# Sixteen pairs of seven block products per layer in place of thirteen, with a third buffer set, in a two-layer decoder trunk

## Chip, cores, metric

The kernel runs on one core of a Trainium2 chip. The metric is the device time of one execution in microseconds. The three timed executions of the kernel before gave 2402.96, 2403.00 and 2404.28 us (median 2403.0).

## What is computed

Two layers over 256 tokens of width 1024. Each layer has a mixer (an input projection, sparse attention with a compressed branch, a gated linear recurrence, a state-space mixer, merge gates, an output projection), and then a retrieval over 128 x 128 single-neuron experts. Cut to what the change touches:

```
x = x + hybrid_mixer(rms_norm(x), ...)
x = x + peer_ffn(rms_norm(x), w_q, sub_keys, u, v)

# inside the mixer, compressed branch:
#   hidden = gelu(blocks @ w1)        (15 blocks a group, 256 hidden columns)
#   k_cmp, v_cmp = hidden @ w2

# peer_ffn: top 16 of 128 x 128 keys for each of 8 heads, gates g
act = gelu(u[eidx] . h)
out = sum over chosen experts of (g * act) * v[eidx]
```

The kernel computes the experts densely. For every token it spreads the gates over all 128 x 128 experts, so that the last product is acts (256 tokens x 16384 experts, mostly zero) times v (16384 x 1024).

## The kernel before

**Products in three passes.** All large products are float32 split in a high and a low part; a product is three matmuls (high by high, high by low, low by high). ScalarE (ACT) makes the high part by a copy with rounding, VectorE (DVE) or GpSimd (POOL) the low part by a subtraction. TensorE (PE) waits for the low part.

**The value stage** is the last stage of a layer. acts times v is cut in 128 units of 128 experts. A plain unit (`value`) is 12 matmuls of 128x512: two token tiles, two column halves, three passes. Its v block comes over `x_load` on the SP queue (512 KB; five slots in turn, so that the load of unit i+4 of the plain units waits until i units are multiplied), then `x_hi` on ACT, then `x_lo` on DVE. The activations of two units are split by `p_hi_pair` and `p_lo_pair`. ACT and DVE each run a loop over i in which they prepare unit i+3; in the loops, every second i begins with a pair split, which on ACT waits until i units are multiplied.

**Seven block products.** A pair of units is a 2 x 2 block matrix product (2 token tiles x 2 units) by (2 units x 2 column halves). For the pairs named in `SEVEN` it is made with seven block products in place of eight: `seven(j)` is 21 matmuls of 128x512 in place of 24. For it four v quarters are loaded (`b_load`, 256 KB each), ACT makes `b_high` and `sums_high`, `a_high`, `a_sums_high`; DVE makes `first_sums`, `last_sums`, `b_low`, `a_sums`, `sums_low`, `a_low`. Tuples such as `FIRST_SUMS` say at which i of the loops each is done, and `SEVEN_AT` before which plain unit PE does the pair. The buffers lie over activations that are used up. Pairs 0 to 2 use set 0 alone (they follow each other at 14 plain units), the others alternate between sets 1 and 0, four plain units apart. `seven_sums`, six steps of DVE at the six plain units after the last pair, add the PSUM banks of the block products to `x`.

There are 13 such pairs a layer and 102 plain units; the last pair comes before plain unit 82.

**The end of layer 0.** SP also issues the first weights of layer 1: `load_first(1)`, the gains, `load_first(0)` and `load_first_rest` (512 KB, the second half of the first weight unit). ACT splits the first unit at the plain unit of number 120 (`one_by_one(120)`, i = 94 of 102), ahead of that i's `x_hi`, and waits there for both halves; DVE makes its low part at i = 96, ahead of that i's `x_lo`. The second unit follows at i = 98 (ACT) and i = 100 (DVE). PE does the last three plain units for token tile 0 first, then `add_sums(0)` on DVE opens the next layer.

**The compressed branch in the mixer.** PE turns the hidden layer (four transposes), does half a unit of projection and eight transposes of q, and then waits for `chT` and `chV`, the turned hidden layer, copied out by ACT. ACT does before that copy: the high part of unit XBC+2, the high part of XBC+3, the copy out of unit XBC+1, and the high part of XBC+4, for which it waits for a load.

Of the kernel before, what the change touches and what calls it, by code (L numbers as in the profile page):

```python
# [24 lines left out]
F32 = mybir.dt.float32  # L25
I32 = mybir.dt.int32
U32 = mybir.dt.uint32
F32R = mybir.dt.float32r
# [82 lines left out]

SEVEN = (7, 15, 23, 26, 29, 32, 35, 38, 41, 44, 47, 50, 53)
SEVEN_SET = (0, 0, 0, 1, 0, 1, 0, 1, 0, 1, 0, 1, 0)
PLAIN = tuple(i for i in range(NKEY) if i // 2 not in SEVEN)
ONE_BY_ONE = len(PLAIN)
SEVEN_AT = tuple(2 * r - 2 * j for j, r in enumerate(SEVEN))
# [13 lines left out]
def slot_free(m):  # L132
# [17 lines left out]
    "seven_loaded_0": 64 * SEVEN_SET.count(0), "seven_loaded_1": 64 * SEVEN_SET.count(1), "seven_hi": 4 * len(SEVEN),  # L150
# [69 lines left out]
def trunk(nc, x_in, pos_tok, pos_row, const, wstream, small, rows, mix_row, ffn_row, subkeys, xstream, out):  # L220
    V, A, PE, PO = nc.vector, nc.scalar, nc.tensor, nc.gpsimd
    with ExitStack() as ctx:
# [3 lines left out]
        def sem(name):  # L226
            return ctx.enter_context(nc.semaphore(name))
# [85 lines left out]
        s_bl = [sem(f"seven_loaded_{i}") for i in range(2)]  # L313
# [7 lines left out]
        def layer_programs(layer):  # L321
# [6 lines left out]
            def past(s):  # L328

                return layer * PER_LAYER[s.name]  # L330
# [133 lines left out]
            with mix:  # L464
# [55 lines left out]
                with mid:  # L520
# [520 lines left out]
                    def mixer_scalar(act):  # L1041
# [106 lines left out]
                        for j in range(2):  # L1148
                            ge = A.activation(chid[j], bank[7][CHAT[j], 0:S], ACT.Gelu_apprx_tanh)
                        ge.then_inc(s_chg, 1)  # L1150
                        for n in range(2, 4):
                            split_hi(act, XBC + n)
                        filler(XBC + 1)
                        act.wait_ge(s_cht, past(s_cht) + 1)
                        A.activation(chT[:], bank[7][:, 0:2 * CROWS].rearrange("p (k c) -> p k c", k=2), ACT.Copy)
                        for k in range(2):
                            for g in range(G):
                                at = k * CROWS + 16 * g
                                rep = A.activation(chV[:, k, g], times(bank[6][:, at:at + NCMP], 8), ACT.Copy)
                        rep.then_inc(s_chtev, 1)  # L1160
                        act.wait_ge(s_cksq, past(s_cksq) + 1)
                        A.activation(kst[:, 0:2], kst[:, 0:2], ACT.Sqrt, scale=1 / DH).then_inc(s_ckrt, 1)
                        filler(XBC + 2)
# [212 lines left out]
                    def mixer_vector(dve):  # L1376
# [165 lines left out]
                        for k in range(CONV):  # L1542
                            lru_conv(k, 0)
                            if k == 0:
                                half_lo(dve, XBC + 1)
                            elif k == 2:
                                split_lo(dve, XBC + 2)
                                q_taken(0)
                                q_taken(1)
                        lru_conv(0, 1)  # L1550
                        split_lo(dve, XBC + 3)

                        dve.wait_ge(s_co, past(s_co) + 1)
                        own = cst[0:8 * NCMP, C_HEAD:C_HEAD + 8].rearrange("p (a g) -> p a g", g=G)
# [537 lines left out]
            with ExitStack() as tmp:  # L2092
# [13 lines left out]
                           for q in range(4)]  # L2106

                unit_at = [acts_at + 4 * i * S for i in range(NKEY)]
                raw_at, sums_at = (feat_at, unit_at[6]), (feat_at + 4 * KT * S, unit_at[14])
                high_at, part_at = (hot_at + 4 * 4 * S, unit_at[22]), (unit_at[0], unit_at[36])  # L2110
                assert high_at[0] + 4 * 7 * 512 <= acts_at
                b_raw = [alias(f"b_raw_{i}", [P, 4, 512], F32, offset=raw_at[i]) for i in range(2)]
                b_lo = [alias(f"b_lo_{i}", [P, 4, 512], F32R, offset=raw_at[i]) for i in range(2)]
                b_sum = [alias(f"b_sum_{i}", [P, 4, 512], F32, offset=sums_at[i]) for i in range(2)]
                b_sum_lo = [alias(f"b_sum_lo_{i}", [P, 4, 512], F32R, offset=sums_at[i]) for i in range(2)]
                b_hi = [alias(f"b_hi_{i}", [P, 7, 512], F32R, offset=high_at[i]) for i in range(2)]
                a_hi = [alias(f"a_hi_{i}", [P, 4, P], F32R, offset=part_at[i]) for i in range(2)]
                a_sum_hi = [alias(f"a_sum_hi_{i}", [P, 4, P], F32R, offset=part_at[i] + 16 * P) for i in range(2)]
                a_sum = [alias(f"a_sum_{i}", [P, 4, P], F32, offset=part_at[i] + 32 * P) for i in range(2)]
                a_sum_lo = [alias(f"a_sum_lo_{i}", [P, 4, P], F32R, offset=part_at[i] + 32 * P) for i in range(2)]  # L2120

                NS = len(SEVEN)
                SHARED = tuple(j == 0 or SEVEN_SET[j] == SEVEN_SET[j - 1] for j in range(NS))
                OTHER_FREE = sum(i < 42 for i in PLAIN)
                OTHER_AFTER = sum(2 * r < 42 for r in SEVEN)
# [12 lines left out]

                def one_by_one(unit):

# [71 lines left out]
                def expert_sync(sp):  # L2212
# [7 lines left out]
                    for m in range(XR, VU + ONE_BY_ONE):  # L2220
                        x_load(sp, m)
                        done = m - XV + 1 - VU
                        if done in (1, 2):
                            sp.wait_ge(s_xu, past(s_xu) + VU + done)
                            for piece in range(2 * done - 2, 2 * done):
                                b_load(0, piece)
                        if done in (OTHER_FREE, OTHER_FREE + 1):
                            sp.wait_ge(s_xu, past(s_xu) + VU + OTHER_FREE)
                            sp.wait_ge(s_bmul, past(s_bmul) + OTHER_AFTER)
                            for piece in range(2 * (done - OTHER_FREE), 2 * (done - OTHER_FREE) + 2):  # L2230
                                b_load(SEVEN_SET.index(1), piece)
# [108 lines left out]
                def expert_scalar(act):  # L2340
# [64 lines left out]
                    def b_high(j):  # L2405

                        b = SEVEN_SET[j]
                        act.wait_ge(s_bl[b], past(s_bl[b]) + 64 * (SEVEN_SET[:j].count(b) + 1))
                        A.activation(b_hi[b][:, 0, :], b_raw[b][:, 0, :], ACT.Copy)
                        A.activation(b_hi[b][:, 1:3, :], b_raw[b][:, 2:4, :], ACT.Copy).then_inc(s_bhi, 1)  # L2410
# [59 lines left out]
                def expert_vector(dve):  # L2470
# [129 lines left out]
                    def first_sums(j):  # L2600

                        b = SEVEN_SET[j]
                        w = b_raw[b]
                        dve.wait_ge(s_bl[b], past(s_bl[b]) + 64 * (SEVEN_SET[:j].count(b) + 1))
                        dch.link(V.tensor_tensor(b_sum[b][:, 0:2, :], w[:, 1:4:2, :], w[:, 0:2, :], ALU.subtract))

# [15 lines left out]
                    def a_sums(j):  # L2622

                        b, unit = SEVEN_SET[j], 2 * SEVEN[j]
                        if j == 0:
                            dve.wait_ge(s_xu, past(s_xu) + VU + 6)
                        a11, a21, a12, a22 = [acts[:, unit + n, t * P:(t + 1) * P] for n in range(2) for t in range(2)]
                        s1, s2, s3, s4 = [a_sum[b][:, n, :] for n in range(4)]
                        dch.add(V.tensor_tensor(s1, a21, a22, ALU.add))
# [234 lines left out]
```

## Time and profile before

| | |
|---|---|
| median of three executions | 2403.0 us |
| profiled execution, its own time | 2402.95 us |
| its span in the trace | 2401.1 us |
| granted TensorE clock, mean | 0.999 of full |
| PE busy | 2379.0 us (99%) |
| DVE busy | 1911.3 us (80%) |
| ACT busy | 1444.8 us (60%) |
| POOL busy | 791.3 us (33%) |
| DMA queue q1 | 416.47 MB, 51.2% of 16 engines |

The difference between the execution's own time and its span (1.85 us) lies around the program. PE busy is no measure of speed, since matmuls overlap and their ends are modelled; the distance from one matmul's start to the next is what counts. The tables below are rows of the page, of the chain of work that ended last, of the timelines of single engines and of the DMA issues. In a timeline a line has its start, its duration, the engine, the line of the kernel, the operation with output and inputs, and in brackets how long the engine was idle before it and who released it.

### The profile page before, as it was taken

The numbers are of one execution on the slowest core, as the hardware profiler recorded it, in microseconds if no ns is written. First come the engines' busy times: TensorE is split into PE (matmuls) and PEld (weight loads), VectorE is DVE, ScalarE is ACT, GpSimd is POOL, SyncE is SP. The second block draws the span as 40 slices with busy tenths as digits, with TensorE's granted clock in tenths as the row PEclk, the third lists the DMA queues.
The fourth block names the chain that finished last, engine by engine and source line by source line (L and its number), as shares of the span: only waits on it lengthen the run. The fifth ranks groups of instructions, "written<-read, shape, count | busy, mean of one in ns | idle before, by whom it ended". The sixth has DMA issues, their size and how long they took to land.

```text
span 2401.1 us, 43695 instructions
## 1 busy us (share of the span) xinstructions
PE 2379.0 (99%) x17453; PEld 2215.8 (92%) x17453; DVE 1911.3 (80%) x3222; ACT 1444.8 (60%) x2123; POOL 791.3 (33%) x452
## 2 busy tenths in 40 slices
PE   9999999999999999999999999999999999999999
PEld 8999999999999988888899999999999999888887
DVE  7988787499389985899779886865984899868995
ACT  6587664444577764665555966644446777656663
POOL 0011310288888820000000113003888989100000
PEclk9999999999999999999999999999999999999999
DMA  7633335355544466666555333453555444566664
GB/s 258 221 124 124 112 140 197 132 185 185 178 159 161 162 204 198 214 201 224 183 193 211 124 124 117 150 184 139 184 180 175 159 161 160 204 203 211 200 192 150
DMA packets 104169, 419.26 MB, mean 175 GB/s; under 512 B 11680, under 2 KB 12192, under 8 KB 87072
## 3 DMA queue, kind: packets, MB, share of 16 engines
q1 hardware_dynamic: 103968, 416.47, 51.2%
q8 instruction: 140, 2.29, 0.4%
q14 instruction: 61, 0.50, 0.1%
HBM read 415.38 MB, written 1.05 MB: 173 GB/s over the span
## 4 chain that ended last, share of the span: by engine, by line
PE 90%; DVE 4%; ACT 3%; DMA 2%; issue 1%; POOL 1%; SPq 0%; DVEq 0%; ACTq 0%
PE banks L2306 23%; PE banks L421 18%; PE banks L422 18%; PE banks L423 18%; PE banks L2287 3%; PE banks L2322 2%; PE banks L2323 2%; PE banks L2321 2%; DVE ring_lo L396 1%; PE banks L881 1%; DMA ring<-in_wstream 1%; POOL xr_lo L1902 1%; DMA xr<-in_xstream 1%; PE banks L768 1%; PE banks L839 1%
## 5 line engine op out<-in xcount | busy, mean ns | idle before, releaser
L1902 POOL TENSOR_TENSOR xr_lo<-xr,xr_hi 128x1024 fp32r<-128x1024 f32 x256 | 621.0, 2429 | 388.0 <-ACT xr_hi L1896 386.7
L1896 ACT ACTIVATE xr_hi<-xr 128x1024 fp32r<-128x1024 f32 x420 | 442.7, 1055 | 282.9 <-DMA xr<-in_xstream 282.2
L421 PE MATMUL banks<-featH,xr_hi 128*128 128x256 f32 x2048 | 576.3, 281 | 1.8 <-POOL xr_lo L1902 1.8
L422 PE MATMUL banks<-featL,xr_hi 128*128 128x256 f32 x2048 | 575.3, 281 | 0.0
L423 PE MATMUL banks<-featH,xr_lo 128*128 128x256 f32 x2048 | 575.2, 281 | 0.0
L421 PEld LDWEIGHTS banks<-featH,xr_hi 128*128 128x128 f32 x2048 | 385.7, 188 | 2.6 <-POOL xr_lo L1902 1.7
L423 PEld LDWEIGHTS banks<-featH,xr_lo 128*128 128x128 f32 x2048 | 386.1, 189 | 0.0
L422 PEld LDWEIGHTS banks<-featL,xr_hi 128*128 128x128 f32 x2048 | 386.1, 189 | 0.0
L421 PE MATMUL banks<-featH,ring_hi 128*128 128x256 f32 x1232 | 351.0, 285 | 2.2 <-DVE ring_lo L396 2.1
L422 PE MATMUL banks<-featL,ring_hi 128*128 128x256 f32 x1232 | 346.2, 281 | 0.0
L423 PE MATMUL banks<-featH,ring_lo 128*128 128x256 f32 x1232 | 345.9, 281 | 0.0
L1317 POOL TENSOR_TENSOR tok_z<-tok_z,rst 128x512 f32<-128x512 f32 (+1 forms) x32 | 51.0, 1593 | 822.1 <-DVE rst L1620 822.1
L396 DVE TENSOR_TENSOR ring_lo<-ring,ring_hi 128x2048 fp32r<-128x2048 f32 x118 | 270.8, 2298 | 58.5 <-ACT ring_hi L388 57.2
L388 ACT ACTIVATE ring_hi<-ring 128x2048 fp32r<-128x2048 f32 x118 | 225.2, 1911 | 90.9 <-PE banks L423 73.2
L1902 DVE TENSOR_TENSOR xr_lo<-xr,xr_hi 128x1024 fp32r<-128x1024 f32 x164 | 200.5, 1222 | 58.2 <-ACT xr_hi L1896 57.4
L421 PEld LDWEIGHTS banks<-featH,ring_hi 128*128 128x128 f32 x1232 | 232.3, 189 | 5.4 <-issue 4.2
L422 PEld LDWEIGHTS banks<-featL,ring_hi 128*128 128x128 f32 x1232 | 232.2, 188 | 0.1
L423 PEld LDWEIGHTS banks<-featH,ring_lo 128*128 128x128 f32 x1232 | 232.2, 188 | 0.0
L2306 PE MATMUL banks<-xr_lo,p_hi 128*128 128x512 f32 x656 | 202.8, 389 | 0.0
L2306 PE MATMUL banks<-xr_hi,p_hi 128*128 128x512 f32 x656 | 202.7, 389 | 0.0
L2306 PE MATMUL banks<-xr_hi,acts_lo 128*128 128x512 f32 x656 | 202.7, 389 | 0.0
L2566 DVE TENSOR_TENSOR hot<-banks,choice 128x1024 fp32r<-128x1024 f32 x128 | 156.6, 1224 | 53.5 <-PE banks L2287 51.6
(424 smaller groups left out, 4962.3 us busy)
## 6 DMA issues: line engine op xcount, KB each, us to landing
xr<-in_xstream SPq DMA_DIRECT2D x420, 512.0 KB, 3.3
ring<-in_wstream SPq DMA_DIRECT2D x128, 1024.0 KB, 4.8
b_raw<-in_xstream SPq DMA_DIRECT2D x104, 256.0 KB, 3.4
xv<-in_xstream SPq DMA_DIRECT2D x40, 512.0 KB, 4.3
smw<-in_small SPq DMA_DIRECT2D x4, 617.0 KB, 9.3
first<-in_wstream SPq DMA_DIRECT2D x4, 512.0 KB, 5.9
first<-in_wstream SPq DMA_DIRECT2D x2, 1024.0 KB, 7.7
subk<-in_subkeys SPq DMA_DIRECT2D x2, 1024.0 KB, 7.0
```

The source lines that it names most:

```text
L388: A.activation(hi, w, ACT.Copy).then_inc(s_hi, 1)
L396: V.tensor_tensor(lo, w, hi.bitcast(F32), ALU.subtract).then_inc(s_lo, 1)
L421: PE.matmul(o, s_hi_lo[0], m_hi_lo[0], start=first, stop=False)
L422: PE.matmul(o, s_hi_lo[0], m_hi_lo[1], start=False, stop=False)
L423: return PE.matmul(o, s_hi_lo[1], m_hi_lo[0], start=False, stop=last)
L1317: PO.tensor_tensor(sc[:, n % 2, :, 0:nk], sc[:, n % 2, :, 0:nk], over(rst[:, n % 2, 2, :], nk), ALU.mult).then_inc(s_scaled, 1)
L1896: A.activation(hi, w, ACT.Copy).then_inc(s_xhi, 1)
L1902: (PO if m < NKEY else V).tensor_tensor(lo, w, hi.bitcast(F32), ALU.subtract).then_inc(s_xlo_pool if m < NKEY else s_xlo_dve, 1)
L2287: mm = PE.matmul(gate_bank(g)[:, 2 * j * P:2 * (j + 1) * P], hots(g)[:, j, 0, :], hots(g)[:, j, 1:3, :], start=True, stop=True)
L2306: mm = PE.matmul(bank[2 * t + h][:], p, w[:, h * 512:(h + 1) * 512], start=first_one and i == 0, stop=last and i == ONE_BY_ONE - 1)
L2321: PE.matmul(bank[o][:], p[0], w[0], start=o >= 4 and j == 0, stop=False)
L2566: V.tensor_tensor(hots(g)[:, :, 0:3:2, :], iota.unsqueeze(1).unsqueeze(1).to_broadcast([P, GB, 2, NKEY]), choice[:, 0:2, GB * g:GB * (g + ...
```

## The change

Sixteen pairs in place of thirteen: pairs follow each other at ten plain units while set 0 is alone (7, 13, 19), then at four (from pair 22). There are 96 plain units, and the last pair comes before plain unit 86. The last pair has a buffer set of its own (set 2). The steps of preparation get places counted from the pair before (`step(alone, start, in_turn)`) in place of `lead`; waits (`used_up`) guard the buffers that now lie over other activations. The loads of the first weights of layer 1 are tied to other pairs. In the compressed branch, ACT copies the turned hidden layer before it splits XBC+3 and XBC+4, and DVE makes the low part of XBC+3 before a step of the recurrence's convolution.

```diff
-SEVEN = (7, 15, 23, 26, 29, 32, 35, 38, 41, 44, 47, 50, 53)
-SEVEN_SET = (0, 0, 0, 1, 0, 1, 0, 1, 0, 1, 0, 1, 0)
+SEVEN = (7, 13, 19, 22, 25, 28, 31, 34, 37, 40, 43, 46, 49, 52, 55, 58)
+SEVEN_SET = (0, 0, 0, 1, 0, 1, 0, 1, 0, 1, 0, 1, 0, 1, 0, 2)
...
                         ge.then_inc(s_chg, 1)
-                        for n in range(2, 4):
-                            split_hi(act, XBC + n)
-                        filler(XBC + 1)
+                        split_hi(act, XBC + 2)
+                        take(XBC + 1, xbcT[:, 2:4, PAD:])
                         act.wait_ge(s_cht, past(s_cht) + 1)
...
                         rep.then_inc(s_chtev, 1)
+                        split_hi(act, XBC + 3)
+                        next_hi(XBC + 1)
                         act.wait_ge(s_cksq, past(s_cksq) + 1)
...
+                        split_lo(dve, XBC + 3)
                         lru_conv(0, 1)
-                        split_lo(dve, XBC + 3)
...
-                raw_at, sums_at = (feat_at, unit_at[6]), (feat_at + 4 * KT * S, unit_at[14])
-                high_at, part_at = (hot_at + 4 * 4 * S, unit_at[22]), (unit_at[0], unit_at[36])
+                raw_at, sums_at = (feat_at, unit_at[6], unit_at[22]), (feat_at + 4 * KT * S, unit_at[14], unit_at[81])
+                high_at = (hot_at + 4 * 4 * S, unit_at[22], unit_at[89])
+                part_at = (unit_at[0], extra_at + 10 * D, unit_at[66])
...
-                def lead(j, units, later):
-
-                    return SEVEN_AT[j] - units if SHARED[j] else SEVEN_AT[j - 1] + later
-
-                B_HIGH = FIRST_SUMS = tuple(lead(j, 11, -2) for j in range(NS))
-                LAST_SUMS = tuple(lead(j, 10, -1) for j in range(NS))
-                SUMS_HIGH = tuple(lead(j, 9, -1) for j in range(NS))
-                B_LOW = tuple(lead(j, 8, -1) for j in range(NS))
-                A_HIGH = A_SUMS = tuple(lead(j, 7, 0) for j in range(NS))
-                A_SUMS_HIGH = SUMS_LOW = tuple(lead(j, 6, 0) for j in range(NS))
-                A_LOW = tuple(lead(j, 4, 0) for j in range(NS))
+                OTHER = SEVEN_SET.index(1)
+
+                def step(alone, start, in_turn):
+
+                    return tuple(SEVEN_AT[0] - 11 + alone if j == 0 else SEVEN_AT[j - 1] + alone if j < OTHER else
+                                 SEVEN_AT[j - 1] + (start if j == OTHER else in_turn) for j in range(NS))
+
+                FIRST_SUMS, B_HIGH = step(1, -2, -2), step(1, -1, -2)
+                LAST_SUMS, SUMS_HIGH = step(2, -1, -1), step(2, 0, -1)
+                B_LOW, A_HIGH, A_SUMS = step(3, 0, -1), step(4, 0, 0), step(4, 0, 0)
+                A_SUMS_HIGH, SUMS_LOW, A_LOW = step(5, 1, 0), step(5, 1, 0), step(6, 1, 0)
+
+                def used_up(eng, unit):
+
+                    eng.wait_ge(s_xu, past(s_xu) + VU + sum(i < unit for i in PLAIN))
+                    eng.wait_ge(s_bmul, past(s_bmul) + sum(2 * r < unit for r in SEVEN))
...
-                            if SEVEN_SET[j] in SEVEN_SET[j + 1:]:
+                            if j + 2 < NS and j + 1 >= OTHER or j + 1 < OTHER:
                                 sp.wait_ge(s_bmul, past(s_bmul) + j + 1)
                                 for piece in range(4):
-                                    b_load(SEVEN_SET.index(SEVEN_SET[j], j + 1), piece)
+                                    b_load(j + 2 if j + 1 >= OTHER else j + 1, piece)
                         if layer + 1 < L:
-                            if done == SEVEN_AT[NS - 1] + 2:
+                            if done == SEVEN_AT[NS - 2] + 2:
                                 programs[layer + 1]["load_first"](sp, 0)
-                            elif done == SEVEN_AT[NS - 1] + 4:
+                            elif done == SEVEN_AT[NS - 1] + 2:
                                 programs[layer + 1]["load_first_rest"](sp)
```

`done` is the number of plain units multiplied. `load_first_rest` is issued at done = 86 of 102 before and at done = 88 of 96 after; ACT splits the first unit at i = 94 of 102 before and at i = 88 of 96 after, DVE at i = 96 and i = 90. The six steps of `seven_sums` lie at i = 83 to 88 before and at i = 87 to 92 after.

## Rows read from the trace of the kernel before

**Rows 1.** Page, part 4: the chain that ended last, by engine.

```profile
PE 90%; DVE 4%; ACT 3%; DMA 2%; issue 1%; POOL 1%; SPq 0%; DVEq 0%; ACTq 0%
```

**Rows 2.** The chain in order of time, value stage of layer 0 (start, us, what).

```profile
863.60 38.09 PE banks L2306 x168
...
992.49 10.91 PE banks L2306 x48
...
1149.52 50.37 PE banks L2306 x222
```

**Rows 3.** Timeline of PE, compressed branch, layer 0 and then layer 1.

```profile
94.05 1.09 PE L744 MATMUL banks<-cst,tok_q 128*128 128x128 f32 x8
94.90 0.36 PE L421 MATMUL banks<-featH,ring_hi 128*128 128x256 f32 x1
...
104.35 1.04 PE L744 MATMUL banks<-cst,tok_q 128*128 128x128 f32 x8
105.45 0.62 PE L792 MATMUL banks<-smw,xbcC 128*15 128x64 f32 x8
...
1297.01 1.04 PE L744 MATMUL banks<-cst,tok_q 128*128 128x128 f32 x8
1298.25 0.62 PE L792 MATMUL banks<-smw,xbcC 128*15 128x64 f32 x8 [0.20 <-ACT xbcC L1159]
```

**Rows 4.** Timeline of ACT, compressed branch, layer 0.

```profile
100.89 0.60 ACT L1075 ACTIVATE xbcT<-banks 128x512 f32<-128x512 f32 x1
102.73 1.92 ACT L388 ACTIVATE ring_hi<-ring 128x2048 fp32r<-128x2048 f32 x1 [1.24 <-DMA ring<-in_wstream]
...
104.65 0.75 ACT L1159 ACTIVATE xbcC<-banks 128x120 f32<-128x120 f32 x4
```

**Rows 5.** Timeline of the SP queue, end of layer 0.

```profile
1118.14 1.75 SPq L2216 DMA_DIRECT2D b_raw<-in_xstream  x4
...
1160.46 0.33 SPq L1886 DMA_DIRECT2D xr<-in_xstream  x1
1160.83 1.20 SPq L364 DMA_DIRECT2D first<-in_wstream  x1
```

**Rows 6.** DMA issues of short windows: KB each, us from issue to landing.

```profile
first<-in_wstream SPq DMA_DIRECT2D x1, 512.0 KB, 5.7
...
first<-in_wstream SPq DMA_DIRECT2D x1, 512.0 KB, 4.4
...
b_raw<-in_xstream SPq DMA_DIRECT2D x2, 256.0 KB, 3.8
```

**Rows 7.** Timeline of ACT, value stage of layer 0.

```profile
1133.55 1.92 ACT L2416 ACTIVATE b_hi<-b_sum 128x2048 fp32r<-128x2048 f32 x1 [4.46 <-DVE b_sum L2612]
...
1182.77 1.90 ACT L388 ACTIVATE first_hi<-first 128x2048 fp32r<-128x2048 f32 x1
1184.57 1.04 ACT L1896 ACTIVATE xr_hi<-xr 128x1024 fp32r<-128x1024 f32 x1
```

**Rows 8.** Timeline of DVE, value stage of layer 0.

```profile
1122.37 0.28 DVE L2629 TENSOR_TENSOR a_sum<-acts 128x128 f32<-128x128 f32 x1
...
1123.43 2.29 DVE L2638 TENSOR_TENSOR b_sum_lo<-b_sum,b_hi 128x2048 fp32r<-128x2048 f32 x1
...
1160.63 0.68 DVE L2665 TENSOR_TENSOR x<-x,banks 128x512 f32<-128x512 f32 x1
...
1161.94 0.69 DVE L2597 TENSOR_TENSOR acts_lo<-acts,p_hi 128x512 fp32r<-128x512 f32 x1
1162.55 1.22 DVE L1902 TENSOR_TENSOR xv_lo<-xv,xv_hi 128x1024 fp32r<-128x1024 f32 x1
1163.68 0.68 DVE L2668 TENSOR_TENSOR x<-x,banks 128x512 f32<-128x512 f32 x1
...
1189.35 2.28 DVE L396 TENSOR_TENSOR first_lo<-first,first_hi 128x2048 fp32r<-128x2048 f32 x1
...
1199.91 1.29 DVE L2714 TENSOR_TENSOR x<-x,banks 128x512 f32<-128x512 f32 x2 [0.59 <-PE banks L2306]
```

More of the change, by code:

```diff
@@ L149 @@
     "expert_weights_loaded_4": 16 * slot_loads(4),
-    "seven_loaded_0": 64 * SEVEN_SET.count(0), "seven_loaded_1": 64 * SEVEN_SET.count(1), "seven_hi": 4 * len(SEVEN),
+    "seven_loaded_0": 64 * SEVEN_SET.count(0), "seven_loaded_1": 64 * SEVEN_SET.count(1), "seven_loaded_2": 64 * SEVEN_SET.count(2),
+    "seven_hi": 4 * len(SEVEN),
     "seven_made": 3 * len(SEVEN), "seven_multiplied": len(SEVEN),
@@ L312, in trunk @@
         s_phi, s_plo, s_xffn = sem("probs_hi"), sem("probs_lo"), sem("x_ffn")
-        s_bl = [sem(f"seven_loaded_{i}") for i in range(2)]
+        s_bl = [sem(f"seven_loaded_{i}") for i in range(3)]
         s_bhi, s_bmade, s_bmul = sem("seven_hi"), sem("seven_made"), sem("seven_multiplied")
@@ L2108, in layer_programs @@
                 unit_at = [acts_at + 4 * i * S for i in range(NKEY)]
-                raw_at, sums_at = (feat_at, unit_at[6]), (feat_at + 4 * KT * S, unit_at[14])
-                high_at, part_at = (hot_at + 4 * 4 * S, unit_at[22]), (unit_at[0], unit_at[36])
-                assert high_at[0] + 4 * 7 * 512 <= acts_at
-                b_raw = [alias(f"b_raw_{i}", [P, 4, 512], F32, offset=raw_at[i]) for i in range(2)]
-                b_lo = [alias(f"b_lo_{i}", [P, 4, 512], F32R, offset=raw_at[i]) for i in range(2)]
@@ L2114, in layer_programs @@
[L2114 to L2118, printed above, removed]
@@ L2119, in layer_programs @@
-                a_sum = [alias(f"a_sum_{i}", [P, 4, P], F32, offset=part_at[i] + 32 * P) for i in range(2)]
-                a_sum_lo = [alias(f"a_sum_lo_{i}", [P, 4, P], F32R, offset=part_at[i] + 32 * P) for i in range(2)]
-                NS = len(SEVEN)
-                SHARED = tuple(j == 0 or SEVEN_SET[j] == SEVEN_SET[j - 1] for j in range(NS))
-                OTHER_FREE = sum(i < 42 for i in PLAIN)
-                OTHER_AFTER = sum(2 * r < 42 for r in SEVEN)
-                def lead(j, units, later):
-                    return SEVEN_AT[j] - units if SHARED[j] else SEVEN_AT[j - 1] + later
@@ new lines, in layer_programs @@
+                high_at = (hot_at + 4 * 4 * S, unit_at[22], unit_at[89])
+                part_at = (unit_at[0], extra_at + 10 * D, unit_at[66])
+                a_sum_at = (unit_at[0] + 32 * P, unit_at[36], unit_at[66] + 32 * P)
+                assert high_at[0] + 4 * 7 * 512 <= acts_at and part_at[1] + 32 * P <= extra_at + 15520
+                b_raw = [alias(f"b_raw_{i}", [P, 4, 512], F32, offset=raw_at[i]) for i in range(3)]
+                b_lo = [alias(f"b_lo_{i}", [P, 4, 512], F32R, offset=raw_at[i]) for i in range(3)]
@@ new lines, in layer_programs @@
+                b_sum = [alias(f"b_sum_{i}", [P, 4, 512], F32, offset=sums_at[i]) for i in range(3)]
+                b_sum_lo = [alias(f"b_sum_lo_{i}", [P, 4, 512], F32R, offset=sums_at[i]) for i in range(3)]
+                b_hi = [alias(f"b_hi_{i}", [P, 7, 512], F32R, offset=high_at[i]) for i in range(3)]
+                a_hi = [alias(f"a_hi_{i}", [P, 4, P], F32R, offset=part_at[i]) for i in range(3)]
+                a_sum_hi = [alias(f"a_sum_hi_{i}", [P, 4, P], F32R, offset=part_at[i] + 16 * P) for i in range(3)]
@@ new lines, in layer_programs @@
+                a_sum = [alias(f"a_sum_{i}", [P, 4, P], F32, offset=a_sum_at[i]) for i in range(3)]
+                a_sum_lo = [alias(f"a_sum_lo_{i}", [P, 4, P], F32R, offset=a_sum_at[i]) for i in range(3)]
+                NS = len(SEVEN)
+                OTHER = SEVEN_SET.index(1)
+                def step(alone, start, in_turn):
+                    return tuple(SEVEN_AT[0] - 11 + alone if j == 0 else SEVEN_AT[j - 1] + alone if j < OTHER else
+                                 SEVEN_AT[j - 1] + (start if j == OTHER else in_turn) for j in range(NS))
@@ L2226, in expert_sync @@
                                 b_load(0, piece)
[L2227 to L2231, printed above, removed]
+                        other = done - SEVEN_AT[OTHER - 1] + 6
+                        if other in (0, 1):
+                            used_up(sp, 14)
+                            for piece in range(2 * other, 2 * other + 2):
+                                b_load(OTHER, piece)
                         if done in SEVEN_AT:
@@ L2407, in b_high @@
                         b = SEVEN_SET[j]
+                        if j == OTHER:
+                            used_up(act, 36)
+                        elif b == 2:
+                            used_up(act, 103)
                         act.wait_ge(s_bl[b], past(s_bl[b]) + 64 * (SEVEN_SET[:j].count(b) + 1))
@@ L2603, in first_sums @@
                         w = b_raw[b]
+                        if j == OTHER:
+                            used_up(dve, 22)
+                        elif b == 2:
+                            used_up(dve, 89)
                         dve.wait_ge(s_bl[b], past(s_bl[b]) + 64 * (SEVEN_SET[:j].count(b) + 1))
@@ L2626, in a_sums @@
                             dve.wait_ge(s_xu, past(s_xu) + VU + 6)
+                        elif j == OTHER:
+                            used_up(dve, 38)
                         a11, a21, a12, a22 = [acts[:, unit + n, t * P:(t + 1) * P] for n in range(2) for t in range(2)]
```

## The prediction, on record before the result

> **What bounds the kernel now.** I read the page's chain first: nine tenths of it are PE [rows 1], so a saving is real only if it shortens PE's own work, and a delay elsewhere counts only where it makes PE wait. Then I followed the chain through the value stage of layer 0. The reader is to see there that nothing but matmuls stands between its start and its end, and that the starts are regular: from 863.60 to 992.49 there are three rounds of 14 plain units and one pair, 42.96 us each; from 992.49 to 1149.52 ten rounds of 4 units and one pair, 15.70 us each [rows 2]. The difference of 27.26 us is ten units, so a unit takes 2.726 us (the last run of 222 matmuls gives 50.37 / 222 x 12 = 2.72) and a pair of seven products 15.70 - 10.90 = 4.80 us. PE is the bound, and ACT, DVE and SP run ahead of it. The third reading is how far ahead, in the timelines of these engines.
>
> **More pairs.** Each new pair takes away two plain units (5.45 us) and adds 4.80 us: 0.65 us less. Three pairs in each of two layers: 6 x 0.65 = 3.9 us gained. The rows are regular over 13 rounds, so I give this term no range, on condition that PE never waits.
>
> **The turned hidden layer.** In layer 0 PE starts eight transposes at 104.35; the same eight took 0.85 us from start to the next work at 94.05. It could go on at 105.20 and does at 105.45; in layer 1 at 1297.86 and does at 1298.25, with ACT's copy named as releaser [rows 3]. ACT's copies end at 105.40 because they stand behind a high part that waited 1.24 us for its load and ran from 102.73 [rows 4]. In the new order they follow the copy out that starts at 100.89, and end near 102.5, well ahead. Gain 0.25 + 0.39 = 0.6 us, from both ends 0 (if the next wait takes it) to 0.6. I take 0.6, since the chain after it is PE's own. The high part of XBC+3 moves to about 102.5 to 104.4, its low part (2.29 us, as the same shape in [rows 8]) ends before 107, and PE, which goes on at 105.2, has 16 small matmuls and half a unit to do before it needs it. DVE only changes the order of two pieces of work. I cost these moves at nothing; without that cover each would cost at most the 1.9 us of the high part.
>
> **The end of layer 0.** This is where I expect the time to go. Count from the moment at which 88 plain units are multiplied. SP then issues a unit's load and, 0.37 us later, `load_first_rest`, as it did at 1160.46 and 1160.83 [rows 5]. That transfer took 5.7 us to land [rows 6], so it lands at 6.1. Before, ACT asked for it eight units after its issue; now ACT asks at i = 88, which it enters at the same moment as SP (its pair split waits for 88 units). So ACT stands from 0.6 to 6.1. Behind that wait are the high part of the first unit (1.80 us to the next instruction) and then `x_hi` of unit 91 (1.04 us) [rows 7]: ready at 8.95. DVE's low part takes 1.22 us [rows 8]: 10.2. PE wants unit 91 after three units, at 8.2. **Stall one: 2.0 us.**
>
> DVE is then late as well. From 1161.94, 1162.55 and 1163.68 a pair split takes 0.61 us and an `x_lo` 1.13 us before the next can start, and a step of `seven_sums` 1.31 us (1160.63 to 1161.94); the low part of the first unit takes 2.28 us [rows 8]. The six steps of `seven_sums` now fall on i = 87 to 92, together with that low part at i = 90. After `x_lo` of unit 91 starts at 9.0, unit 92 is ready at 9.0 + 1.13 + 1.31 + 1.22 = 12.7, in time for PE at 12.9. Unit 93 must wait for a step, a pair split and the low part: its `x_lo` starts at 11.4 + 1.13 + 1.31 + 0.61 + 2.28 = 16.8 and ends at 18.0, and PE wants it at 10.2 + 5.45 = 15.65. **Stall two: 2.3 us.** The last three units are done for tile 0 first, half a unit (1.36 us) each, while DVE needs 1.13 + 1.31 = 2.44 us for each: **stalls three and four, 1.1 us each.** Then a last step of sums and the low part of the second unit (another 2.28 us) stand before `add_sums(0)`: DVE is free at about 25.6 and PE's sums of tile 0 are there at 24.2. Before, `add_sums` started at 1199.91, where the last run of matmuls ends in the chain [rows 2, 8]. **A delay of 1.4 us** on the chain into layer 1. Together 2.0 + 2.3 + 1.1 + 1.1 + 1.4 = 7.9 us, in layer 0 only. The other landing of such a transfer was 4.4 us [rows 6], which takes 1.3 us off the first term: 6.6 us. Layer 1 has neither the load nor the splits, and I cost its end at nothing: without the wait DVE's work on i = 87 to 92 fits in the two units by which it is ahead.
>
> The Trainium skill (DMA: Bandwidth & Descriptors, section on the anatomy of one DMA) puts a transfer at about 2.0 us plus its bytes over 436 GB/s, 3.2 us for 512 KB. The two landings here, 5.7 and 4.4 us, are longer. By the page's figure ACT would be through at 6.5, unit 91 in time, and the end of the layer would cost about 5.5 us in place of 7.9, the whole sum 2.4 us less.
>
> **While set 0 is alone.** For pairs 1 and 2 the quarters can be loaded only when the pair before is multiplied, and the preparation now starts one unit after it and not three. Count from the end of that pair. Four issues take 1.75 us [rows 5], the last starts at 1.3 plus 0.2 for the semaphore, and lands 3.8 us later [rows 6]: 5.3. ACT's `b_high` (a p and an x shape, 1.5), pair split (0.5) and `x_hi` (1.04): 8.4. DVE's `x_lo` 1.22 and last sums 1.3: 11.0. ACT's `sums_high` 1.92 and next `x_hi` 1.04 [rows 7]: 13.95. From there DVE has no wait but much work: `x_lo` three times before the last (3.39), `b_low` 1.74, two pair splits 1.22, `a_sums` 1.06 (1122.37 to 1123.43), `sums_low` 2.2, and the `x_lo` of the ninth unit on 1.22 [rows 8]: 24.8. PE wants that unit after nine units, 24.5. That is 0.3, and with the semaphore steps I left out 0.4. Two such places in each layer: 1.6 us. From both ends: 0 if DVE is half a microsecond quicker, 0.9 us each (3.6) if the quarters land later. Pair 0 is prepared up to a unit earlier than it was but with the same work; layer 0's slower loads may add 0.3. In the stretch where sets alternate, the places of the work are those of before, and the rounds of 15.70 held; the third set only gives the last pair its own buffers, and its waits are for units used up long before. No cost.
>
> **Sum.** -3.9 - 0.6 + 7.9 + 1.6 + 0.3 = +5.3 us. The profiled execution took 2402.95 us, the median is 2403.0, so the sum is made against the same figure: 2408.3 us, 0.22% more. A change of 0.2% (4.8 us) is about what a measurement of this kernel tells from none.
>
> **Rivals.** *The end is cheap.* If the rest of the first weights lands before ACT needs it, or DVE makes its steps faster, only stalls two to four are left, or part of them: 4.5 + 1.6 + 0.3 + 0 to 2 - 4.5, between 2404 and 2406.5. For it speaks the 4.4 us landing, against it that DVE's part follows from its own rows. *No stall at the end and none between pairs* (the other side): PE then keeps its regular starts and the whole gain stays, 2403.0 - 4.5 = 2398.5, or 2400 with the 1.6. It decides from the point at which unit 91 is ready at 8.2, so the load must land by 4.1, and DVE must also be done with unit 93 by 13.6. Against it stands every row used above. *DVE and ACT become the bound.* A round of four units and one pair costs DVE nearly PE's 15.70 us; if the preparation of pairs 1 and 2 is later than I think, its delay is kept through all later rounds, each pair waits, and the upper ends hold (3.6 and more): 2410.5 to 2415. For it speaks that ACT and DVE wait for each other inside a round (4.46 us idle in [rows 7]), against it that in the 13 rounds of [rows 2] no pair waited.
>
> **Chances.** Forecast, 2406.5 to 2410.5: 0.57. Cheap end: 0.16. No stall: 0.13. DVE bound: 0.14. Slower by over 0.2% (above 2407.8) is some two thirds of the first case and all of the last: 0.52. Faster by over 0.2% (below 2398.2) needs the no-stall case and a little more: 0.05. Within: 0.43. Range 2401.5 to 2412.0; the likeliest case's own is 2406.5 to 2410.5.
>
> **What would show it.** In the trace after: rounds of 15.70 us unchanged; in the value stage of layer 0 a PE gap of 2 us three units after `load_first_rest` is issued, with ACT's high part of the first unit waiting some 5 us for a DMA; a second gap two units later, released by DVE; `add_sums` late behind the low part of the second unit; layer 1 without all that; small PE gaps nine units after pairs 0 and 1. The hidden layer's matmuls follow the transposes at 0.85 us. The prediction is wrong if ACT reaches i = 88 with the load landed, or if PE's rounds are broken elsewhere.

## The result, and the profile after

The kernel after took 2410.8 us in the median of seven executions (2408.3 to 2415.1), the kernel before on the same chip 2404.25 us: ratio 1.0030, 95% interval 1.0018 to 1.0041. It is slower, by an interval that lies clear of 1. Measured once more beside the experiments on another chip, it was 2412.2 against 2403.4 us: 1.0036 (1.0022 to 1.0049). The profiled execution took 2408.31 us with a span of 2406.4 us, 5.3 us more than the one before.

The chain of the kernel after in the value stage of layer 0 (start, us, what) answers to [rows 2]:

```profile
863.44 32.69 PE banks L2311 x144
896.21 5.94 PE banks L2311 x24
...
932.10 2.97 PE banks L2311 x12
939.92 10.93 PE banks L2311 x48
...
972.46 10.91 PE banks L2311 x48
...
1176.58 10.89 PE banks L2311 x48
1188.84 1.05 ACT xr_hi L1898
1189.91 1.23 DVE xr_lo L1904
...
1195.55 2.28 DVE first_lo L397
1197.84 1.14 DVE xr_lo L1904
...
1204.51 2.29 DVE first_lo L397
1206.80 1.20 DVE x L2729 x2
```

Three stretches are to be seen. From 972.46 to 1176.58 there are thirteen rounds of 15.70 us, as before: PE never waits. Up to 972.46 the chain leaves PE, where it did not in [rows 2]. At the end the chain goes through ACT and DVE. The waits of PE by line and releaser (us in total, times, longest) say what for; before, the value matmuls were not in this list:

```profile
PE banks L2311 <- DVE xr_lo L1904: 5.6, 8, 2.1
...
PE banks L2311 <- DVE xv_lo L1904: 0.8, 1, 0.8
```

**The end of layer 0.** The SP queue, then ACT, then DVE, then those lines of PE that have a wait:

```profile
1182.42 0.43 SPq L365 DMA_DIRECT2D first<-in_wstream  x1
```

```profile
1187.02 1.92 ACT L389 ACTIVATE first_hi<-first 128x2048 fp32r<-128x2048 f32 x1 [4.33 <-DMA first<-in_wstream]
1188.84 1.98 ACT L1898 ACTIVATE xr_hi<-xr 128x1024 fp32r<-128x1024 f32 x2
```

```profile
1189.91 1.23 DVE L1904 TENSOR_TENSOR xr_lo<-xr,xr_hi 128x1024 fp32r<-128x1024 f32 x1 [6.43 <-ACT xr_hi L1898]
...
1195.55 2.28 DVE L397 TENSOR_TENSOR first_lo<-first,first_hi 128x2048 fp32r<-128x2048 f32 x1
1197.76 1.22 DVE L1904 TENSOR_TENSOR xr_lo<-xr,xr_hi 128x1024 fp32r<-128x1024 f32 x1
...
1204.51 2.29 DVE L397 TENSOR_TENSOR first_lo<-first,first_hi 128x2048 fp32r<-128x2048 f32 x1
1206.72 1.28 DVE L2729 TENSOR_TENSOR x<-x,banks 128x512 f32<-128x512 f32 x2
```

```profile
1191.28 0.70 PE L2311 MATMUL banks<-xr_hi,p_hi 128*128 128x512 f32 x2 [1.11 <-DVE xr_lo L1904]
1199.12 0.71 PE L2311 MATMUL banks<-xr_hi,p_hi 128*128 128x512 f32 x2 [2.14 <-DVE xr_lo L1904]
1201.57 0.70 PE L2311 MATMUL banks<-xv_hi,p_hi 128*128 128x512 f32 x2 [0.83 <-DVE xv_lo L1904]
1204.03 0.70 PE L2311 MATMUL banks<-xr_hi,p_hi 128*128 128x512 f32 x2 [0.83 <-DVE xr_lo L1904]
```

ACT waits 4.33 us for the load issued at 1182.42, and `x_hi` of the next unit stands behind it. DVE is idle for 6.43 us and from then on busy without a break to `add_sums` (L2729). PE has the four waits of the forecast. From start to start, against 2.72 us a unit and 1.36 us for half a unit, they cost more than the idle time in the bracket: 1201.57 - 1199.12 - 1.36 = 1.1 us for the third (0.83 in its bracket), and 1199.12 - 1191.28 - 5.44 = 2.4 us for the second. The four together are 1.3, 2.4, 1.1 and 1.1 us. `first_lo` (L397) is DVE's low part of a first weight unit; the second one keeps `add_sums` back: 1206.72 - 1204.03 - 1.36 = 1.3 us. From the stage's first matmul to `add_sums`: before 1199.91 - 863.60 = 336.31 us, after 1206.72 - 863.44 = 343.28.

**How the losses are read off in every run.** With sixteen pairs and without any wait the stage would take 336.31 - 3 x 0.65 = 334.36 us up to `add_sums`, and 34 units and three pairs, 107.1 us, up to the first round of 15.70. What is above 107.1 is the loss while set 0 is alone; the rest above 334.36 is the loss at the end. For the kernels with thirteen pairs the whole is 336.31 us, and for those with pairs 14 units apart the first part is that of the kernel before. In layer 0 of the kernel after: 972.46 - 863.44 - 107.1 = 1.9 us, and 343.28 - 334.36 - 1.9 = 7.0 us (the five pieces above make 7.2; the two readings agree to 0.2). In layer 1 the stage starts at 2062.58 and the round at 2171.84: 2.2 us, and nothing at the end. The 1.9 + 2.2 us of the kernel after divide by place, from the first matmul behind one pair to that behind the next: 0.6 and 0.8 us (layers 0 and 1) up to pair 0, and 0.8, 0.5, 0.6 and 0.8 us behind pairs 0 and 1 of the two layers. The profiled executions of all kernels, in us:

| kernel | set 0 alone, layer 0 + layer 1 | end of layer 0 | median, minus before on the same chip |
|---|---|---|---|
| after | 1.9 + 2.2 | 7.0 | +6.6 |
| after, again | 3.5 + 2.9 | 7.1 | +8.8 |
| rest of the weights three units earlier | 2.0 + 3.2 | 2.6 | +3.9 |
| first weights loaded and split ahead | 2.3 + 2.7 | 0.0 | +0.5 |
| last sums one place earlier | 0.0 + 0.0 | 7.4 | +2.8 |
| the last two together | 0.0 + 0.0 | 0.1 | -5.0 |
| thirteen pairs, ten units apart | 3.0 + 1.7 | 0.0 | +4.5 |
| kernel before, rest issued at 94 | 0 + 0 | 4.3 | +1.6 |
| kernel before, turned hidden layer first | 0 + 0 | 0.0 | -0.1 (one execution) |

### The profile page after: what moved, and what is told of

Same layout as the page of the kernel before. It is cut to its first block, busy times and chain, and to the rows that moved or that the text cites. A ratio compares the mean times of both kernels' runs of the same rounds, so it can differ in the third digit from the quotient of the medians.

```text
span 2406.4 us, 43727 instructions
## 1 busy us (share of the span) xinstructions
PE 2377.4 (99%) x17435; PEld 2209.9 (92%) x17435; DVE 1942.4 (81%) x3276; ACT 1450.1 (60%) x2135; POOL 791.1 (33%) x452
## 4 chain that ended last, share of the span: by engine, by line
PE 85%; DVE 7%; ACT 3%; issue 2%; DMA 2%; POOL 0%; SPq 0%; ACTq 0%; DVEq 0%
PE banks L422 18%; PE banks L424 18%; PE banks L423 18%; PE banks L2311 17%; PE banks L2292 3%; PE banks L2327 2%; PE banks L2328 2%; PE banks L2326 2%; DVE ring_lo L397 1%; DVE xr_lo L1904 1%; PE banks L882 1%; DMA xr<-in_xstream 1%; PE banks L840 1%; PE banks L859 1%; DMA xv<-in_xstream 1%
## 5 line engine op out<-in xcount | busy, mean ns | idle before, releaser
L1898 ACT ACTIVATE xr_hi<-xr 128x1024 fp32r<-128x1024 f32 x410 | 431.5, 1053 | 238.5 <-DMA xr<-in_xstream 238.0
L397 DVE TENSOR_TENSOR ring_lo<-ring,ring_hi 128x2048 fp32r<-128x2048 f32 x118 | 270.8, 2298 | 58.2 <-ACT ring_hi L389 56.8
L1904 DVE TENSOR_TENSOR xr_lo<-xr,xr_hi 128x1024 fp32r<-128x1024 f32 x154 | 187.5, 1221 | 43.4 <-ACT xr_hi L1898 42.3
L2311 PE MATMUL banks<-xr_hi,p_hi 128*128 128x512 f32 x616 | 191.6, 391 | 5.7 <-DVE xr_lo L1904 5.6
L2311 PE MATMUL banks<-xr_lo,p_hi 128*128 128x512 f32 x616 | 190.5, 389 | 0.0
L2311 PE MATMUL banks<-xr_hi,acts_lo 128*128 128x512 f32 x616 | 190.4, 389 | 0.0
```

What stands on the lines that cost most here:

```text
L397: V.tensor_tensor(lo, w, hi.bitcast(F32), ALU.subtract).then_inc(s_lo, 1)
L1898: A.activation(hi, w, ACT.Copy).then_inc(s_xhi, 1)
L1904: (PO if m < NKEY else V).tensor_tensor(lo, w, hi.bitcast(F32), ALU.subtract).then_inc(s_xlo_pool if m < NKEY else s_xlo_dve, 1)
L2311: mm = PE.matmul(bank[2 * t + h][:], p, w[:, h * 512:(h + 1) * 512], start=first_one and i == 0, stop=last and i == ONE_BY_ONE - 1)
```

## The experiments

**The rest of the first weights three units earlier.** All of the kernel after, but the second half of the first weight unit is issued at 85 multiplied units, not 88.

```diff
-                            elif done == SEVEN_AT[NS - 1] + 2:
+                            elif done == SEVEN_AT[NS - 1] - 1:
```

> The kernel after with one number changed: the rest of the first weights of layer 1 is issued at 85 plain units, not 88. If the late landing sets off the stalls at the end of layer 0 (my theory), ACT has the data when it reaches i = 88, the gap of PE before unit 91 goes, and DVE's own work leaves about 1.1 us of the four gaps that sum to 5.6 us, while the sums of layer 1's input stay about 1.4 us late: some 4.5 us less than the kernel after, near 2406 us or 0 to 0.1% over before. If DVE's crowded work at i = 87 to 92 is enough by itself (rival), three of the gaps (4.3 us) stay and only 1.3 us comes back.

Measured: 2407.1 us, ratio to the kernel before 1.0014 (1.0005 to 1.0023). That is 3.9 us over the kernel before on the same chip, where the kernel after lay 6.6 us over it on its own chip (8.8 us when it was measured again): 2.7 to 4.9 us less. ACT and DVE in this kernel:

```profile
1183.46 0.63 ACT L2408 ACTIVATE p_hi<-acts 128x512 fp32r<-128x512 f32 x1 [5.45 <-PE banks L2311]
1184.00 1.91 ACT L389 ACTIVATE first_hi<-first 128x2048 fp32r<-128x2048 f32 x1
```

```profile
1192.52 2.28 DVE L397 TENSOR_TENSOR first_lo<-first,first_hi 128x2048 fp32r<-128x2048 f32 x1
...
1201.48 2.29 DVE L397 TENSOR_TENSOR first_lo<-first,first_hi 128x2048 fp32r<-128x2048 f32 x1
1203.69 1.28 DVE L2729 TENSOR_TENSOR x<-x,banks 128x512 f32<-128x512 f32 x2
```

The split has no wait for a load, and the end costs 2.6 us in place of 7.0. So 4.4 us hang on the late load. The other 2.6 do not: PE still waits before two of the last three units (0.16 and 0.85 us idle, at 1198.54 and 1200.99), and `add_sums` still stands directly behind the second low part, 1.3 us late.

**First weights loaded and split ahead.** Both loads at 80 multiplied units, ACT's splits at i = 84 and 92 in place of 88 and 92, DVE's low parts at 86 and 93 in place of 90 and 94.

```diff
-                            if done == SEVEN_AT[NS - 2] + 2:
+                            if done == 80:
                                 programs[layer + 1]["load_first"](sp, 0)
-                            elif done == SEVEN_AT[NS - 1] + 2:
                                 programs[layer + 1]["load_first_rest"](sp)
...
-                        if layer + 1 < L and i in (one_by_one(120), one_by_one(124)):
-                            programs[layer + 1]["split_hi"](act, i // one_by_one(124))
+                        if layer + 1 < L and i in (84, 92):
+                            programs[layer + 1]["split_hi"](act, i // 92)
...
-                        if layer + 1 < L and i in (one_by_one(122), one_by_one(126)):
-                            programs[layer + 1]["split_lo"](dve, i // one_by_one(126))
+                        if layer + 1 < L and i in (86, 93):
+                            programs[layer + 1]["split_lo"](dve, i // 93)
```

> The kernel after with the whole first unit loaded at 80 plain units, its high part at i = 84, its low part at i = 86, the low part of the second unit at i = 93. My theory: no gap of PE is left at the end of layer 0 and the sums are not late, 7 us less than the kernel after; what is left is the gain of the pairs less the stalls while set 0 is alone, about 2403 to 2405 us, level with before. Rival, that the extra time comes from the greater number of pairs (DVE, or the DMA queues, too slow in the rounds of four units): the rounds grow beyond 15.70 us and most of the 6.6 us stays.

Measured: 2403.8 us, ratio 1.0001 (0.9992 to 1.0010), 0.5 us over the kernel before where the kernel after was 6.6 to 8.8 us over it. The rounds of 15.70 us are unchanged, so the rival with too many pairs is out. `add_sums` waits for PE again:

```profile
1201.14 1.28 DVE L2728 TENSOR_TENSOR x<-x,banks 128x512 f32<-128x512 f32 x2 [0.82 <-PE banks L2310]
```

The whole loss at the end is gone, with the same six steps of sums in the same places: they cost nothing with the first low part ahead of them and no wait for a load on ACT. Which of the moved pieces took away the last 2.6 us was not tried one by one.

**Last sums one place earlier.** In the kernel after, DVE's `last_sums` come right behind `first_sums` while set 0 is alone, ahead of a pair split and an `x_lo`; `b_low` moves with them.

```diff
-                LAST_SUMS, SUMS_HIGH = step(2, -1, -1), step(2, 0, -1)
-                B_LOW, A_HIGH, A_SUMS = step(3, 0, -1), step(4, 0, 0), step(4, 0, 0)
+                LAST_SUMS, SUMS_HIGH = step(1, -1, -1), step(2, 0, -1)
+                B_LOW, A_HIGH, A_SUMS = step(2, 0, -1), step(4, 0, 0), step(4, 0, 0)
```

> The kernel after with LAST_SUMS moved from the second to the first unit and B_LOW from the third to the second after the pair before, while set 0 is alone. My theory: ACT's sums_high waits for last_sums, which stand behind a unit's x_lo, and holds back the next x_hi; with the sums made first, the gaps of PE before and around units 13, 23 and 33 go in both layers, about 4 us less than the kernel after, near 2407 us. Rival, that the quarters simply land too late for ten units between pairs: the gaps stay, since the loads are unchanged, and the time is that of the kernel after.

Measured: 2406.1 us, ratio 1.0009 (1.0000 to 1.0018). DVE behind the first pair, in the kernel after and then in this one (L2618 first sums, L2624 and L2625 last sums):

```profile
915.64 1.23 DVE L1904 TENSOR_TENSOR xv_lo<-xv,xv_hi 128x1024 fp32r<-128x1024 f32 x1 [0.32 <-ACT xv_hi L1898]
916.78 0.68 DVE L2624 TENSOR_TENSOR b_sum<-b_raw,b_sum 128x512 f32<-128x512 f32 x1
917.50 0.69 DVE L2625 TENSOR_TENSOR b_sum<-b_raw,b_sum 128x512 f32<-128x512 f32 x1
921.12 1.22 DVE L1904 TENSOR_TENSOR xr_lo<-xr,xr_hi 128x1024 fp32r<-128x1024 f32 x1 [2.93 <-ACT xr_hi L1898]
```

```profile
912.98 1.23 DVE L2618 TENSOR_TENSOR b_sum<-b_raw 128x1024 f32<-128x1024 f32 x1 [4.63 <-DMA b_raw<-in_xstream]
914.24 0.69 DVE L2624 TENSOR_TENSOR b_sum<-b_raw,b_sum 128x512 f32<-128x512 f32 x1
914.97 0.69 DVE L2625 TENSOR_TENSOR b_sum<-b_raw,b_sum 128x512 f32<-128x512 f32 x1
```

In the kernel after DVE finishes the last sums at 918.2, ACT takes 2.9 us for their high part and the next `x_hi`, and DVE stands idle for 2.93 us. With the sums earlier that time is used, and the chain shows the three stretches of plain units whole again:

```profile
864.51 38.09 PE banks L2311 x168
...
907.45 27.23 PE banks L2311 x120
...
939.54 27.23 PE banks L2311 x120
...
971.63 10.91 PE banks L2311 x48
```

All loss while set 0 is alone is gone in both layers, though the quarters are loaded as late as before, so the rival (late quarters) is out. The end of layer 0 costs as much as in the kernel after (7.4 us).

**Both together.** The last two edits in one kernel.

> Both edits together. If the two places are all that stands against the pairs, PE runs through the value stages without a gap: 2403 to 2404 less 3.9 us for six pairs and 0.6 us for the hidden layer, about 2399.5 us, ratio to before 0.998. If other waits take their place, the time stays at or above 2403.

Measured: 2398.3 us (2397.2 to 2401.0) against 2403.3, ratio 0.9980 (0.9971 to 0.9989). This version beats both kernels, the one before by 5.0 us and the one after by 12 to 14 (6.6 + 5.0 and 8.8 + 5.0, each taken against the kernel before on its own chip). The value matmuls are not in the list of PE's waits any more; the chain has the three stretches and then

```profile
1175.20 23.13 PE banks L2310 x102
1198.36 1.29 DVE x L2728 x2
```

From the stage's start at 863.94 to `add_sums` that is 334.42 us, the 334.36 that three pairs more should give. This is the measurement of the gain itself: about 1.9 us a layer from the pairs, 3.9 of the 5.0 us. Where the other 1.1 us come from is not shown; they lie within the interval (2.6 to 7.0 us).

**Kernel before, the rest issued where it is asked for.** The kernel before with its thirteen pairs; only the second half of the first weight unit is issued at 94 multiplied units, where ACT splits, in place of 86.

```diff
-                            elif done == SEVEN_AT[NS - 1] + 4:
+                            elif done == SEVEN_AT[NS - 1] + 12:
```

> The kernel before, thirteen pairs, with one thing changed: the second half of layer 1's first weight unit is issued at the same place at which ACT asks for it (94 plain units multiplied, not 86). Theory: the wait for the late load alone costs one gap of PE, 1.3 to 2.0 us, before unit 97 (ACT waits 4.3 to 5.5 us, then the high part, the unit's x_hi, DVE's x_lo), since by then the six steps of sums (i = 83 to 88) are done; whether the low part at i = 96 makes a second gap of up to 1 us is open; add_sums for token tile 0 not more than 1 us late. Time +1.5 to +3 us on the kernel before, 2404.8 to 2406.3. Rival (the wait for the load is the whole cost of the end, sums and low parts cost nothing by themselves): +5 us and more here too, 2408.5. Second rival (the landing is hidden): no gap, 2403.4.

Measured: 2405.1 us (2403.9 to 2408.4), ratio 1.0008 (0.9999 to 1.0017): the median is where it was forecast, but not to be told from nothing. In its profile ACT waits 5.69 us for the load, and PE waits once, 2.46 us, somewhat longer than forecast. Yet `add_sums` comes 4.3 us later than before, where at most 1 us was forecast: 2.4 us are the wait, and the other 1.9 us are PE's clock. In the table each line has the stretch and its length, PE's busy time and matmuls, the granted clock, and last the DMA share and GB/s:

```profile
1190.00:1192.00 2.00, 0.36 (x2) 1.00 0.47 127
1192.00:1194.00 2.00, 1.18 (x4) 0.81 0.53 199
1194.00:1196.00 2.00, 2.00 (x7) 0.50 0.04 8
1196.00:1198.00 2.00, 2.00 (x9) 0.83 0.00 0
1198.00:1200.00 2.00, 2.00 (x11) 1.00 0.00 0
```

```profile
1192.82 0.82 PE L2306 MATMUL banks<-xr_hi,p_hi 128*128 128x512 f32 x2 [2.46 <-DVE xr_lo L1902]
1193.43 1.05 PE L2306 MATMUL banks<-xr_lo,p_hi 128*128 128x512 f32 x2
1194.29 1.05 PE L2306 MATMUL banks<-xr_hi,acts_lo 128*128 128x512 f32 x2
```

After the wait two matmuls take 0.86 us from start to start, and 0.45 at the full clock. So the wait alone, with the sums already over, makes one gap and not four, and the first rival's +5 us in the median did not come. The 4.3 us of this one profile look like that rival, but 1.9 of them are the clock; how often the clock fell in the other ten executions is not known.

**Thirteen pairs, ten units apart.** The code after with only its first thirteen pairs and without the third buffer set.

```diff
-SEVEN = (7, 13, 19, 22, 25, 28, 31, 34, 37, 40, 43, 46, 49, 52, 55, 58)
-SEVEN_SET = (0, 0, 0, 1, 0, 1, 0, 1, 0, 1, 0, 1, 0, 1, 0, 2)
+SEVEN = (7, 13, 19, 22, 25, 28, 31, 34, 37, 40, 43, 46, 49)
+SEVEN_SET = (0, 0, 0, 1, 0, 1, 0, 1, 0, 1, 0, 1, 0)
```

> The code after, with only the first thirteen of its pairs (pairs 1 and 2 ten units after the one before; no third buffer set), so that the last pair, the loads and splits of layer 1's first weights and the sums lie far apart again. Theory: PE waits only while set 0 is alone, about 2 us in each layer, and the hidden layer gives 0.6 back: +3.4 us on the kernel before, 2406.7 (2405.7 to 2407.7); no PE gap behind unit 90 of layer 0, add_sums right behind PE. Rival (pairs ten units apart cost nothing, all of the loss is the end): 2402.7, no PE wait for x_lo.

Measured: 2407.9 us, ratio 1.0019 (1.0010 to 1.0028), 0.2 us above the upper end of the expectation. The pairs ten units apart, with their steps in the places of the kernel after, make a slower kernel without any loss at the end; the experiment with the last sums shows that it is the places and not the distance. The end costs nothing here: in the chain 318 matmuls of plain units run without a break from 1130.57, and `add_sums` follows them at once, at 1202.72.

**The kernel after, again.**

> The kernel after once more, beside the other kernels of this group on the same chip: 2409 to 2411, ratio 1.002 to 1.003 to the kernel before, with the same gaps.

Measured: 2412.2 us, above the expected 2411. At the end of layer 0 the first two waits are there (1.13 and 2.15 us idle); then PE runs at a granted clock of 0.50 from 1202 to 1204, so that the third wait has no idle time and the fourth only 0.26 us. The end costs 7.1 us all the same. While set 0 was alone it lost 6.4 us in place of 4.1, with a wait seven units after pairs 0 and 1 (926.27 and 960.00) besides that nine units after them. So that term differs between two profiles of one kernel, taken on two chips.

**The turned hidden layer alone, in the kernel before.** ACT's copy ahead of the high part of XBC+3, DVE's low part ahead of the convolution's step.

```diff
-                        for n in range(2, 4):
-                            split_hi(act, XBC + n)
-                        filler(XBC + 1)
+                        split_hi(act, XBC + 2)
+                        take(XBC + 1, xbcT[:, 2:4, PAD:])
...
+                        split_hi(act, XBC + 3)
+                        next_hi(XBC + 1)
```

> The kernel before with only the compressed branch's order changed (the turned hidden layer is copied out ahead of the high part of XBC+3, the low part of XBC+3 ahead of the convolution's step). Theory: the matmuls that use the turned layer follow the eight transposes at 0.85 us in both layers (before 1.10 and 1.24), 0.6 us less in all, which a single time can't tell from nothing. Rival (the next wait takes the gain): they start earlier, and the norm or the score stage behind them starts no earlier.

Measured: 2403.3 us once, with 2403.4 before; as expected, nothing to be told. PE in its layer 0:

```profile
105.81 1.04 PE L744 MATMUL banks<-cst,tok_q 128*128 128x128 f32 x8
106.78 0.62 PE L792 MATMUL banks<-smw,xbcC 128*15 128x64 f32 x8
```

The turned layer is used 0.97 us after the transposes start, not 0.85; in layer 1 too (1298.29 to 1299.26). The matmuls that follow differ from those at 94.05 in [rows 3], from which I had the 0.85. So PE goes on 0.13 + 0.27 = 0.4 us earlier at this place. That it reaches the total is not shown: the value stage of layer 0 starts at 863.60 and 863.63 in the two profiles with the old order, and between 863.38 and 865.05 in the eight with the new one. The rival that a later wait takes the gain stays open.

## Why the prediction was right, and where its sum was not

**Result.** The direction, the place and the mechanism were right: 2408.3 was forecast, 2410.8 and 2412.2 were measured, inside the range of 2401.5 to 2412.0 the first time and 0.2 us above it the second. The likeliest case's own range (to 2410.5) was missed by 0.3 us. That the profiled execution came to 2408.31 is luck: the value stages give -3.9 + 4.1 + 7.0 = +7.2 us, and 1.9 us less in the rest make the 5.3 of the profile. Of these 1.9 us, 1.7 lie between `add_sums` and the value stage of layer 1, which took 857.59 us before and 855.86 after, but 857.55 when the kernel after was profiled again. So that part moves by 1.7 us by itself and hid a term that was too small.

**More pairs, -3.9 us.** Shown. The rounds kept 15.70 us, and the kernel with both repairs has the stage of layer 0 at 334.42 us.

**Turned hidden layer, -0.6 us.** At most 0.4 us, by the eight transposes' 0.97 us in place of 0.85, and not shown to reach the total.

**End of layer 0, +7.9 us.** 7.0 us in the same five pieces: 1.3, 2.4, 1.1, 1.1 and 1.3 for 2.0, 2.3, 1.1, 1.1 and 1.4. Only stall one was clearly off: the load issued at 1182.42 released ACT at 1187.02, after 4.6 us and not 5.7. The terms are not separate costs: the first edit showed that 4.4 us go with the late load, and the second that the places of the loads and splits decide on the rest. The formula of the Trainium skill (DMA: Bandwidth & Descriptors, Anatomy of one DMA) is fitted to transfers issued by way of GpSimd, which the prediction did not say, and these loads go over the SP queue. The estimate from it, 3.2 us for this load, would have put the end at 5.5 us. The trace, with 4.6 us, lies between it and the row that I took, and at 7.0 us the end does too.

**While set 0 is alone, +1.6 and +0.3 us: the step that was mis-sized.** It cost 4.1 us in the profile after and 4.7 to 6.4 in the other four profiles with this spacing and these steps. The two parts of the term were both too small. The four places behind pairs 0 and 1 were put at 1.6 us and cost 2.7 (3.1 to 4.5 in the other four, where 3.6 was named as the upper bound). The way up to pair 0 was put at 0.3 us for slower loads in layer 0, and cost 1.3 (1.2 to 1.9), in layer 1 as well (0.8). For the places behind the pairs the working followed one unit, the ninth, and for that it nearly held. PE's next start behind pair 0, that `x_lo`, and PE's start on the unit:

```profile
906.84 0.62 PE L2311 MATMUL banks<-xv_hi,p_hi 128*128 128x512 f32 x2
...
930.73 1.22 DVE L1904 TENSOR_TENSOR xr_lo<-xr,xr_hi 128x1024 fp32r<-128x1024 f32 x1
...
932.10 0.70 PE L2311 MATMUL banks<-xr_hi,p_hi 128*128 128x512 f32 x2 [0.40 <-DVE xr_lo L1904]
```

`x_lo` was forecast to be over 24.8 us after the pair and was over after 25.1 (931.95 - 906.84); PE wanted it after 24.5. PE's idle time of 0.40 us is the forecast one, but the place cost 0.8 us: here too the wait cost more than its idle time. And I asked it of one unit alone: PE also waited just ahead of pair 0 (896.21, and 2095.51 in layer 1), and in some executions seven units after a pair. By the prediction's own list of signs, the breaks ahead of pair 0 are rounds broken at a place that it did not name. That the order of DVE's steps makes all of this loss is shown by the edit that brings its sums forward; why one execution loses 4.1 us and another 6.4 was not separated.

**The rivals.** A cheap end did not come: the landing was early enough to shorten one stall, but DVE's queue held. (Its sum was added up wrongly: 4.5 + 1.6 + 0.3 + 0 to 2 - 4.5 us on 2403 is 2404.9 to 2406.9, not 2404 to 2406.5.) "DVE or ACT is the bound" gave a time near the measured one, yet its mechanism is refuted: no lateness was carried into the later rounds, where thirteen rounds of 15.70 us follow, and the loss stayed where it arose. "No stall" is what the two repairs made: 2398.5 was its time, 2398.3 the measured one. Its -4.5 us counts 0.6 for the hidden layer that no run confirms, so the close agreement is in part luck.

## What to carry to other kernels

When the number of steps in a schedule changes, list what each in-order engine has between two fixed events, and look for the instruction behind which everything queues: here a wait for a load of 4.3 us on ACT, and an idle time of 2.9 us on DVE made by the order of two of its own steps. A saving on the bounding engine counts only once every preparing engine is ahead again; the same sixteen pairs were 0.3% slower or 0.2% faster than thirteen, by the places of two loads, of the splits of two units, and of the last sums with the low part behind them. In a working with slack near zero, follow every unit, not only the one that looks worst.

## Not expected of the hardware

A wait of PE can cost more than its own length, by the clock. In the kernel before with the rest issued at 94, PE had been idle for 2.46 us, and the granted clock then was 0.50 (1.2 of 2.4 GHz) between 1194 and 1196 and full again from 1198: 1.9 us lost on top. When the kernel after was profiled again, a wait of 2.15 us was followed by a clock of 0.61 from 1200 to 1204; in its first profile a wait of 2.14 us at the same place left the clock at 1.00. There the drop cost nothing, since DVE set the pace: from the first round of 15.70 to `add_sums` the two took 234.3 and 234.4 us. The drop in the first case is part of why its eleven times spread over 4.5 us, but that is argued and not shown.

The load of the weight half (512 KB) released ACT 4.6 us after its issue in both profiles of the kernel after; by the traces it landed after 4.5 us there and 5.9 us in the kernel before with the late issue.
